# A two-block transformer kernel on one core: the query and key-value expansions of the second block take turns, and the SP queue issues the rotary exchange

## The reference, cut to what matters

```python
proj = h @ w_in                                    # second block's input projection
c_q  = rmsnorm(proj[..., cq columns]);  c_kv = rmsnorm(proj[..., ckv columns])
k_rope = rope(proj[..., kr columns], positions)
q_b  = c_q  @ w_uq      # 384 -> 8 heads x (128 nope + 64 rope)
kv_b = c_kv @ w_ukv     # 128 -> 8 heads x (128 nope + 128 v)
q_rope = rope(q_b[..., 128:], positions)           # x1*cos - x2*sin, x2*cos + x1*sin
s = (q_nope . k_nope + q_rope . k_rope) * scale; p = softmax(causal(s)); o_b = p @ v
mix = concat([o_a, o_b])                           # o_a: 16 heads of 64, sliding window
x = x + g1 * (mix @ w_out)                         # w_out: 2048 x 2048
```

## Time and profile before

| | |
|---|---|
| time, median of 3 (lowest, highest) | 2105.72 us (2105.41, 2106.75) |
| the profiled execution, its own time | 2106.19 us |
| span of the profile | 2104.4 us |
| PE busy | 2087.5 us, 99% |
| DVE busy / ACT busy | 1510.9 us, 72% / 1059.3 us, 50% |
| DMA | 506.39 MB, mean 241 GB/s |
| mean granted TensorE clock | 0.998 of 2.4 GHz |

### The profile page before, as it was taken

The page is one execution under the profiler, slowest core; times in us unless marked ns, Lnnn a source line. Parts: engine busy times, 40 slices in busy tenths (PEclk is TensorE's granted clock), DMA queues, the critical chain, the costliest instruction groups (busy, mean ns, idle before and its releaser), DMA issues.

```text
span 2104.4 us, 29119 instructions
## 1 busy us (share of the span) xinstructions
PE 2087.5 (99%) x11332; PEld 1797.1 (85%) x11332; DVE 1510.9 (72%) x2009; ACT 1059.3 (50%) x1534; POOL 18.4 (1%) x34
## 2 busy tenths in 40 slices
PE   9999999999999999999999999999999999999998
PEld 8888888888888888888888898888888888888887
DVE  6869666788989888898766766577555555556555
ACT  6654555554444434444456666565443444344443
POOL 0000000000000000000000000000000000000000
PEclk9999999999999999999999999999999999999999
DMA  8787335788888999988765525455555555555553
GB/s 335 274 309 268 133 101 177 287 317 324 325 330 339 362 368 349 339 328 341 304 250 185 201 87 190 170 215 195 194 188 196 186 198 188 192 193 187 197 183 121
DMA packets 75096, 506.39 MB, mean 241 GB/s; under 512 B 8730, under 2 KB 9226, under 8 KB 17104
## 3 DMA queue, kind: packets, MB, share of 16 engines
q1 hardware_dynamic: 70992, 488.67, 63.3%
q0 software_dynamic: 2864, 14.55, 1.8%
q10 hardware_dynamic: 1104, 1.31, 0.2%
HBM read 501.79 MB, written 2.18 MB: 239 GB/s over the span
## 4 chain that ended last, share of the span: by engine, by line
PE 96%; DVE 2%; ACT 1%; DMA 0%; issue 0%; ACTq 0%; DVEq 0%; SPq 0%
PE region L1156 40%; PE region L1090 30%; PE region L1094 16%; PE region L1145 2%; PE bank L1239 1%; PE bank L1196 1%; PE region L1146 1%; PE bank L1205 1%; PE bank L1129 1%; ACT m_WHI L1522 1%; PE bank L1252 1%; DMA m_RAW<-in_nsa_w_in 0%; PE bank L1182 0%; PE bank L1228 0%; ACT m_SP L1608 0%
## 5 line engine op out<-in xcount | busy, mean ns | idle before, releaser
L1909 DVE TENSOR_TENSOR m_WLO<-m_RAW,m_WHI 128x1024 fp32r<-128x1024 f32 (+3 forms) x729 | 867.7, 1204 | 479.5 <-ACT m_WHI L1522 451.8
L1522 ACT ACTIVATE m_WHI<-m_RAW 128x1024 fp32r<-128x1024 f32 (+3 forms) x729 | 751.8, 1042 | 668.5 <-PE region L1156 311.9
L1156 PE MATMUL region<-m_WHI,m_HL 128*128 128x512 f32 x1152 | 361.3, 395 | 0.5 <-DVE m_HL L2113 0.5
L1090 PE MATMUL region<-m_HL,m_WHI 128*128 128x512 f32 x1472 | 357.4, 393 | 0.0
L1090 PE MATMUL region<-m_H,m_WHI 128*128 128x512 f32 x1376 | 328.7, 391 | 0.0
L1090 PEld LDWEIGHTS region<-m_HL,m_WHI 128*128 128x128 f32 x1472 | 269.5, 188 | 52.1 <-issue 0.3
L1090 PEld LDWEIGHTS region<-m_H,m_WHI 128*128 128x128 f32 x1376 | 252.8, 188 | 48.9
L1156 PEld LDWEIGHTS region<-m_WHI,m_HL 128*128 128x128 f32 x1152 | 212.8, 188 | 43.2 <-issue 1.4
L1945 DVE CUSTOM_DVE_ANT_0 m_RAW<-m_RAW,m_CROW,m_consts 128x2048 f32<-128x2048 f32 x96 | 225.2, 2345 | 0.2 <-DMA m_RAW<-in_w_mod 0.2
L1156 PE MATMUL region<-m_WLO,m_HL 128*128 128x512 f32 x576 | 224.6, 390 | 0.0
L1156 PE MATMUL region<-m_WHI,m_HIDL 128*128 128x512 f32 (+1 forms) x512 | 198.3, 387 | 0.0
(11 more groups left out here) (335 smaller groups left out, 1749.4 us busy)
## 6 DMA issues: line engine op xcount, KB each, us to landing
m_RAW<-in_w_ff SPq DMA_DIRECT2D x124, 1024.0 KB, 4.8
m_RAW<-in_w_mod SPq DMA_DIRECT2D x96, 1024.0 KB, 6.6
m_RAW<-in_ffn_w_in SPq DMA_DIRECT2D x88, 1024.0 KB, 6.4
m_RAW<-in_ffn_w_out SPq DMA_DIRECT2D x44, 1024.0 KB, 6.7
m_RAW<-in_nsa_w_in SPq DMA_DIRECT2D x36, 1024.0 KB, 5.8
m_RAW<-in_nsa_w_out SPq DMA_DIRECT2D x16, 1024.0 KB, 4.9
m_RAW<-in_w_out SPq DMA_DIRECT2D x16, 1024.0 KB, 5.0
m_RAW<-in_w_first SPq DMA_DIRECT2D x8, 1024.0 KB, 4.9
```

The lines of the kernel that those rows point to most:

```text
L1090: mm = e.matmul(region[s["reg"]][:, b, :], hi[:, i, c:c + 128], both[:, k + a + i, :, :].rearrange("p a s -> p (a s)"), start=k + a + i == ...
L1156: mm = e.matmul(o, lhs, rhs, start=start and i == 0, stop=fin and i == 2, skip_group_check=True)
L1522: e.activation(WHI[u % 4][:, 0:(z - a) * ncol], raw[:, a * ncol:z * ncol], ACT.Copy).then_inc(a_hi, 1)
L1909: e.tensor_tensor(WLO[u % 4][:, 0:m], raw[:, a * ncol:z * ncol], WHI[u % 4][:, 0:m].bitcast(F32), ALU.subtract).then_inc(v_lo, 1)
```

## The change

The order of slabs becomes uq0, uq1, ukv0, uq2, ukv1, uq3, ukv2, ukv3. The exchange DMAs leave ACT's stream and are issued by the SP queue: the first four ahead of load 331 (now the weights of uq3), the other four ahead of load 335 (out24[0:4]). `rope 0` and `rope 1` become steps of the attention in the first output slab, and the attention's list gets four more steps there (`rope 0`, two empty ones, `rope 1`). Heads 21 to 23 are split from the bank, as heads 24 to 31 are.

```diff
+EXPANSIONS = [(1, 0), (1, 1), (0, 0), (1, 2), (0, 1), (1, 3), (0, 2), (0, 3)]
...
-    for s in uq + ukv:
-        queue(s)
+    uq, ukv, expansions = [], [], []
+    for what, j in EXPANSIONS:
+        made = (make_uq if what else make_ukv)(j)
+        (uq if what else ukv).append(made)
+        expansions.append(made)
+        queue(made)
...
-            side.append(s1)
+            if at + i == 24:
+                side.extend([lambda: put("rope", 0), None, None, s1, lambda: put("rope", 1)])
+            else:
+                side.append(s1)
...
-                    if st["parts"] >= hl_free(x, k) and (x == "h2" or k >= 8):
+                    if st["parts"] >= hl_free(x, k):
...
+    def exchange(i):
+        P.swap_at[len(P.loads)] = i
+
+    P.swap_at = {}
     later.append(("latent",))
-    hook(uq[2], 1, put, "swap", 0)
-    hook(uq[3], 1, put, "rope", 0)
-    hook(ukv[0], 0, put, "swap", 1)
-    hook(out2[0], 1, put, "rope", 1)
-    run(*uq)
+    hook(ukv[0], 0, exchange, 0)
+    hook(ukv[2], 0, exchange, 1)
+    run(*expansions[0:2])
     drain()
-    run(*ukv)
+    run(*expansions[2:])
...
-            elif name == "swap":
-                i, = arg
-                w.wait_ge(*freed("uq", 2 * i + 1))
-                w.wait_ge(v_shift, 8)
-                for p in range(0, 128, 32):
-                    e.dma_start(qsw[p:p + 32, 2 * i:2 * i + 2, :], qrT[p ^ 32:(p ^ 32) + 32, 2 * i:2 * i + 2, :]).then_inc(l_swap[i], 16)
...
+            if n in P.swap_at:
+                pair = P.swap_at[n]
+                own = slice(2 * pair, 2 * pair + 2)
+                w.wait_ge(*freed("uq", 2 * pair + 1))
+                w.wait_ge(v_shift, 8)
+                for p in range(0, 128, 32):
+                    e.dma_start(qsw[p:p + 32, own, :], qrT[p ^ 32:(p ^ 32) + 32, own, :]).then_inc(l_swap[pair], 16)
             if n >= NRAW:
```

More of the change, by code:

```diff
@@ L215, in uq_columns, with make_uq, make_ukv @@
         return nope + rope
-    uq = [slab("uq", j, "w_uq_2", 0, 3, 0, 384,
+    def make_uq(j):
+        return slab("uq", j, "w_uq_2", 0, 3, 0, 384,
                [("f", 0, 0, 0, S), ("f", 128, 0, 256, S), ("f", 256, 1, 0, S)], "cq", per=3,
-               cols=uq_columns(j))
-          for j in range(4)]
-    ukv = [slab("ukv", j, "w_ukv_2", 0, 1, 512 * j, 512,
+                    cols=uq_columns(j))
+    def make_ukv(j):
+        return slab("ukv", j, "w_ukv_2", 0, 1, 512 * j, 512,
                 [("f", 0, 0, 0, S), ("f", 256, 0, 256, S), ("v0", 0, 1, 0, 256), ("v1", 0, 1, 256, 256)], "ckv", per=1)
-           for j in range(4)]
-    for s in uq + ukv:
-        queue(s)
+    uq, ukv, expansions = [], [], []
[4 more added lines that the diff above has]
+        queue(made)
     out2 = down("out2", "w_out_2", 0, KT, "h5", True)
```

## The result

| | before | after |
|---|---|---|
| time, median of 5 (lowest, highest) | 2105.92 us (2105.41, 2108.24) | 2118.36 us (2117.86, 2119.63) |
| the profiled execution, its own time | 2106.19 us | 2117.86 us |
| span | 2104.4 us | 2116.0 us |
| mean granted TensorE clock | 0.998 | 0.996 |

The change makes the kernel slower: the ratio is 1.0059, 95% interval 1.0045 to 1.0072, or 12.4 us between the medians. The forecast was 2115.8, the range 2107 to 2122.

A forecast was written before the change was run, and what follows sets the result against it. PE, busy 99% of the span, was taken as the bound. New losses 3.45 + 1.5 + 1.1 + 7.3 + 1.6 + 0.1 = 15.05 less old 4.9 gave +10.1 us, median 2115.8 us; range 2107 to 2122.

The forecast's parts named there:

- What bounds: PE, busy 99% of the span, bounds the kernel; its losses from 1255.29 to 1300.89, 4.9 us, are the most winnable.
- First exchange: Before load 331: SP waits for uq1's qrT, then issues 2.45 us; uq3 starts 3.45 us late, plus 1.5 clock.
- Behind it: After uq3: out20 needs the region that knT of ukv2 frees, and starts 1.1 us late.
- Second exchange: Before load 335, landing in 4.8 us: rope 0 queues behind its splits; scores of head 24 start 7.3 us late.
- The clock behind the third gap: After the gap before scores of head 24: a half-clock period as before, 1.6 us.
- Attention two tiles later, the gate: Four more attention steps: heads' tiles lose nothing; the later gate row costs DVE about 1.1 us, PE 0.1.
- Sum: Over the whole change: new losses 15.05 us, old ones 4.9, so +10.1 us, median 2115.8 us.
- The rule on issuing engines: For the exchange on SP: issuing costs little, so both issue spans drop, giving +7.1 us rather than +10.1.
- A: uq3's weights come in time, only the exchange before load 335 costs: +3.9 to +5.0, 2109.6 to 2110.7 us; chance 0.12.
- B: Faster: the SP queue holds nothing back, load 335 lands by 1267.9; all 4.9 us won, 2100.8 us; chance 0.09.
- C: Output projection's loads stay late, the 8.8 us landing repeats or grows, DVE's backlog reaches further heads: beyond 2122; chance 0.06.

The follow-up runs named there:

- 5: Kernel before, with only heads 21 to 23 split straight from the bank: 2105.56 us, ratio 0.9998.
- experiment 1: Changed kernel, SP keeps the waits for the evacuations but issues no exchange; the rotation multiplies qrT itself by the sine: 2111.11 us, ratio 1.0024.
- 12: Changed kernel, exchange waits on SP moved ahead of loads 335 and 338, the eight exchange DMAs not issued, rotation from qrT itself: 2103.66 us, ratio 0.9988.
- experiment 6: Kernel before, with only rope 0 and rope 1 moved into the first output slab's attention, plus two empty steps: 2113.29 us, ratio 1.0035.
- 7: Kernel before, with only the exchanges moved from ACT to the SP queue, ahead of loads 330 and 334: 2114.56 us, ratio 1.0038.
- 9: Kernel before, with rotations and four more steps in the first output slab, and heads 21 to 23 split from the bank: 2108.57 us, ratio 1.0013.
- 2: Changed kernel, exchanges still on SP but ahead of loads 335 and 338: 2105.74 us, ratio 0.9999.
- 3: Changed kernel, exchanges issued by POOL's queue, nothing on SP: 2104.17 us, ratio 0.9993.
- 4: Changed kernel, exchanges issued in ACT's stream again, behind ukv0's and ukv2's matmuls: 2107.13 us, ratio 1.0003.
- 8: Changed kernel, exchange issued by POOL, rope 0 and rope 1 back in their old places without extra steps: 2102.63 us, ratio 0.9986.

## Why the prediction was right, point by point

- *What bounds.* Right: PE's waits in 1255 to 1300 carry the whole difference. The start of scores 24 is a landmark: 1289.38 after; by the prediction 1288.7, in the time of the kernel before. The stretch ran 0.64 us earlier in the trace of after (uq1's qrT ends at 1259.04 and not 1259.67), so the like number is 1290.0: 1.3 late against the forecast.
- *First exchange.* Forecast: load 331 issued 2.5 behind the evacuation, lands in 3.7, PE 3.45 late. Measured: 3.0 behind it (four issues, 2.92), 3.84, PE 4.0 late (3.86 of idle time). The issue term was too small by 0.5: one of the four took 1.03. The clock fell, and cost what was forecast: from 1268.09 to the start of the 19th matmul at 1271.72 are 3.63 us in place of 2.16, 1.5 more. That it fell was in part luck, since behind gaps of 2.5 us it fell in the trace of before and not in that of 5.
- *Behind it.* Forecast 1.1 late, measured 1.2 (1.05 of idle time).
- *Second exchange.* The mechanism and the names of every link were right. Mis-sized: the landing of load 335, 5.4 where 4.8 was taken (4.84 in experiment 1, where no exchange goes ahead of it). PE was 7.9 late (7.8 of idle time) where 7.3 stood. The prediction put the 8.8 of the earlier trace rows down to the megabytes in flight; the four exchange transfers were issued beside that load too, from 1266.28 on the earlier trace rows, and 12 shows what they can do. Which of the two made the 8.8 was not tried.
- *The clock behind the third gap.* This is the largest mis-sized term: 1.6 forecast, by likeness to the short gap of before. Measured: from scores of head 24 at 1289.38 over a tile and a turn to the start of the values at 1295.32 PE takes 5.94 us; the same pieces take 3.12 before (1276.96 to 1280.08), so it is 2.8. PE's busy time agrees: 1.5 + 2.8, less the 1.55 of before, is 2.75, and it grew by 2.7. The step that failed is "a clock period as before comes with it": how long the half clock lasts behind a restart is not given by the one before, nor by the length of the gap. It lasted 3.4 us behind a gap of 2.55 (before), 6.0 behind 2.9 (experiment 6), 3.2 behind 3.9 (after), 4.0 behind 5.9 (7) and 5.8 behind 7.8 (after).
- *Attention two tiles later, the gate.* Forecast: 1.1 of waiting on DVE, 0.1 of it on PE. Measured: 0.82 on DVE, nothing more than before on PE. "Nothing" for the heads' tiles was right only because of another part of the change: without the bank split the same step costs 3.6 us and a clock drop (6 against 9). The prediction credited the bank split with 0.65 and did not see that it also pays for the added steps; the total did not suffer, since both are in the change.
- *Sum.* Forecast +10.1. The errors add up and hardly cancel: later scores +1.3, clock +1.2, gate −0.1, and −0.64 because this trace entered the stretch earlier. That makes +11.9, against 11.7 between the profiled executions. The forecast, 2.6 us below the median measured, was in its range because the mechanism was right, with three terms too small: the issues, the landing and the clock.
- *The rule on issuing engines* (the Trainium skill, DMA: Bandwidth & Descriptors, section Issuing engines are not separate DMA queues) would have dropped the issue spans. The prediction gave +7.1 for that, which is a slip: +7.1 is its lower bound, with issues of 0.33 each and a landing of 3.3. Both spans of 2.45 taken out of its sum leave +5.2. Experiment 1, which drops them together with the transfers, measured +5.3 and the full change +12.4. For four small transfers ahead of a load that is already late, the issue time is not small: 2.9 us of issues against a landing of 3.8.
- *The rivals.* A (uq3's weights in time) is refuted by the 3.9 us gap. B (faster) would need nothing held back. In experiments 2 to 4, where the issues have left that place, the loss is gone, but no win can be measured; only 8, with the rotations back as well, wins 3.2 of the 4.9. C (out2's loads slow) did not decide in the change: loads 335 to 338 were asked for at once and took 5.4 to 11.2 us, but PE was already late and waited for none behind the first. A load of 8.4, 8.5 and 7.1 us did appear in 2, 3 and 8; in 2 the cause is another than C's, the exchange in flight beside it (12), and in 3 and 8 that is argued by likeness.

## What to carry to other kernels

An in-order queue that brings weights can take foreign DMAs only where their wait is already met and the next load has slack of the wait, the issues (0.6 us each here) and a landing; otherwise use a queue that nothing is waiting behind, here POOL's. That spares the wait and the issues, not the traffic: beside the exchange from POOL the load still took 8.5 us (3). A part that is worth nothing alone (the bank split) can be what makes another part free, so experiments with single parts of a bundle are read together with at least one pair. What the half clock costs behind one gap is not to be carried over to another: it was 1.5 us behind 3.9 and 2.8 behind 7.8, and it lasted six microseconds behind a gap of only 2.9 (6). A forecast needs a range for it, from nothing up.

## What was not expected of the hardware

- After a gap of 3.9 us PE was at the 1.2 GHz level for about three microseconds, after one of 7.8 for nearly six, and after one of 2.9 in experiment 6 for six. A gap of 1.9 us was followed by a granted clock of 0.50 in the profiled execution of 3 and by 1.00 in that of 2, both before ukv3; a gap of 2.5 before ukv2 by 0.50 in that of before and by 1.00 in that of 5. So gaps of this size bring the drop in some profiled executions and not in others.
- Four 64 KB transfers between buffers on the chip, in flight beside a 1 MB load, took its landing from 4.8 to 8.4 us and the rate from 1264 to 1268 from 381 and 393 to 250 and 221 GB/s (in the first of the two windows there was also less asked for). I had counted only their issues.
- Four such issues take 2.4 to 4.3 us on SP and ACT (4.3 in the profiled execution of 2), 2.0 on POOL. In the first set one of the four took 1.0 to 2.4 us in most traces, but not in that of 4; why was not tried. A load's issue takes 0.33 to 0.7, once 1.6 (in 1).
